# Two-block transformer kernel: the one-column shift products move to TensorE, and the opening's loads and matmuls are reordered

## The chip, the cores and the metric

The kernel runs on one core of one Trainium2 chip. The metric is the device time of one execution in microseconds (us), lower is better.

## What is computed

Two model blocks on one sequence of 512 tokens and width 1024, all in float32. The change touches only the entry of the first block, where a condition vector `c` of 1024 numbers modulates the input:

```
mod = jax.nn.silu(c) @ w_ada[layer] + b_ada[layer]
shift, scale, gate = jnp.split(mod[:, None, :], 3, axis=-1)
h = rms_norm(x, norm_g[layer]) * (1.0 + scale) + shift
proj = h @ w_in[layer]
```

`w_ada` is 1024 x 3072, so shift, scale and gate have 1024 numbers each. Behind it follow HGRN2 and retention heads, an output product, and the second block (convolution, banded attention, two gated feed-forward layers, norms).

## The kernel before, in words

Activations lie with the feature in the partition: x is eight input blocks (`KC` = 8) of 128 features by 512 tokens, in tile `x`. Each f32 product is made of three fast ones: an operand is split into a rounded high part and the rest, its low part, and TensorE adds high x high, low x high and high x low into one bank (the lines of `dense`, L1354 to L1356). So every input block needs `xa_hi` and `xa_lo`, and every weight tile (128 x 1024, half a megabyte) needs `w_hi` and `w_lo`.

Weight tiles come in a fixed order through four slots (`SLOTS`). SyncE loads slot j again once its low part is made (`load`, L376), ScalarE makes the high part (`w_high`, L480), GpSimd the low part (`w_low`, L416), and TensorE uses the tile with all eight input blocks into bank j of `gps`. Each engine's order is written out by hand; nothing is scheduled by a planner. A semaphore is all that ties engines together, and each engine executes its own list strictly in order.

The opening, up to the loop over head pairs:

- SyncE issues in one queue: x's first half, modulation piece 0, x's second half, pieces 1 and 2, weight tile 0, piece 3, tile 1, piece 4, tile 2, pieces 5 to 7, tile 3, constants. A modulation piece is 1 MB and holds, for one input block, the weights of its scale and of its shift, both turned so that an output feature is a partition. ScalarE's queue loads `c` spread over all partitions (`c_wide`) and the table of vectors `vec`.
- ScalarE squares the input blocks (L499), TensorE sums them over the features with a matrix of ones (L1392), ScalarE makes the inverse root `rstd` (L504, L505).
- VectorE makes silu(c) wide (L892), then for each block in `modulation(c)` two products with a running sum over 1024 elements (L897), scale and shift, and the gain (L901); `scaled_input(c)` is x times gain times `rstd` (L910). The first three scaled inputs stand behind the third block's products.
- ScalarE adds the shift in place (L533) and copies the rounded high part (L534), with the high parts of weight tiles 0 to 2 put in between.
- GpSimd makes the low part of input blocks 0 to 5 (L423) and of weight tiles 0 to 2 (L416) in turns; VectorE makes the low part of blocks 6 and 7 (L916). The semaphore `x_ready` counts finished blocks.
- TensorE has weight tiles 0 to 2 in work at once: for blocks 0 to 4 one group of three matmuls per tile and block, then blocks 5 to 7 of tile 0, of tile 1, of tile 2. Then tile 3, and the products of the first head pair.

The first head pair then runs ScalarE's sigmoid of tiles 0 to 3 (L583, L587; the first stands behind two table loads), VectorE's forget gate, key and clamp (L1044, L1047, L1048), ScalarE's log (L590), VectorE's running sums (L1055) and level exponents (L960 to L963), ScalarE's exponentials and copies (L552 to L613), and further weight tiles. TensorE goes from tile 3 to token matmuls (L1383), tiles 6 and 7, the level products (L1451), and the next token matmuls, which need two weight tiles whose low parts GpSimd makes late.

Of the kernel before, what the change touches and what calls it, by code (L numbers as in the profile page):

```python
# [16 lines left out]
F32 = mybir.dt.float32  # L17
# [113 lines left out]
def program(nc, weights, ada_in, c_in, xT, vec_in, sinks_in, rel_in, ret_tab, lvl_in, eye_in, tri_in, hot_in, ident_in,  # L131
            rel_scratch, outT):
    ctx = ExitStack()
    with ctx:
        def sb(name, shape, dt=F32, where=ctx):
            return where.enter_context(nc.sbuf_tensor(name, shape, dt))

        def sem(name):
            return ctx.enter_context(nc.semaphore(name))
# [17 lines left out]
        eps_col = sb("eps_col", [P, 1])  # L157
        mod = sb("mod", [P, 3 * KC])
        conv_gain = sb("conv_gain", [P, KC])
        r_col = sb("r_col", [P, 2, NT])  # L160
        sq = sb("sq", [P, 2, T])
        lnv = sb("lnv", [P, T])
# [78 lines left out]

        gps = ctx.enter_context(nc.psum_tensor("gps", [P, SLOTS, T], F32))
        aps = ctx.enter_context(nc.psum_tensor("aps", [P, 4, T], F32))

# [21 lines left out]
        made = sem("made")  # L266
        lb_shift = sem("lb_shift")
        lb_exp = sem("lb_exp")
        mod_ready = sem("mod_ready")

        sq_ready = sem("sq_ready")
        sq_used = sem("sq_used")
# [61 lines left out]
        def vcol(name, c=0):  # L334
            return vec[:, VEC[name] + c:VEC[name] + c + 1]
# [37 lines left out]
        @block.sync  # L373
        def _(sp):
            def load(I, j):
                sp.dma_start(w_raw[:, j, :], weights[bass.ds(I * SLOTS + j, 1)].rearrange("a p c -> p (a c)"))\  # L376
                  .then_inc(raw_in[j], 16)

            for c in range(KC):  # L380
                if c < 2:
                    k = slice(c * KC // 2, (c + 1) * KC // 2)
                    sp.dma_start(x0[:, k, :], xT.rearrange("(k p) t -> p k t", p=P)[:, k, :]).then_inc(x_in[c], 16)
# [24 lines left out]
        def _(pool):  # L408
# [64 lines left out]
        def _(act):  # L473
# [35 lines left out]
                nc.scalar.mul(dst[:, c, :], res[:, c, :], gain(c)).then_inc(xh_ready, 1)  # L509

            act.dma_start(c_wide[:, 0, :], c_in.to_broadcast([P, D])).then_inc(c_loaded, 16)
            act.dma_start(vec[:], vec_in).then_inc(vec_loaded, 16)

            nc.scalar.preload_act_table(ACT.Sigmoid)
            for c in range(KC):
# [3 lines left out]
                if c == KC // 2 - 1:  # L521
# [318 lines left out]
        def _(dve):  # L840
# [30 lines left out]
            def gain_low(b, c, gain, hi, lo):  # L871
# [16 lines left out]
            own.done(TT(conv_gain[:], vec[:, VEC["final_g"]:VEC["final_g"] + KC], vec[:, VEC["norm_mix"]:VEC["norm_mix"] + KC],  # L888
                        ALU.mult))

            dve.wait_ge(c_wide_ready, 1)
            own.done(TT(c_wide[:, 0, :], c_wide[:, 0, :], c_wide[:, 1, :], ALU.mult))  # L892

            def modulation(c):
                dve.wait_ge(ada_loaded[c], 16)
                for n, col in ((2 * c, KC + c), (2 * c + 1, c)):
                    own.mark(nc.vector.tensor_tensor_reduce(  # L897
                        ada_w[:, n, :], ada_w[:, n, :], c_wide[:, 0, :], op0=ALU.mult, op1=ALU.add, scale=1.0,
                        scalar=vcol("b_ada", col), accum_out=mod[:, col:col + 1]))
                own.wait()  # L900
                own.mark(STT(mix_gain[:, c:c + 1], mod[:, KC + c:KC + c + 1], 1.0, vcol("norm_g", c), ALU.add, ALU.mult))  # L901

            def scaled_input(c):

                if c == 0:
                    dve.wait_ge(rstd_ready, RMS_MIX + 1)
                if c >= 4:
                    dve.wait_ge(x_ready, c - 3)
                own.wait()
                STT(hbuf[:, c % 4, :], x0[:, c, :], mix_gain[:, c:c + 1], rstd[:], ALU.mult, ALU.mult).then_inc(h_ready, 1)  # L910

            def input_low(c):

                dve.wait_ge(xh_ready, c + 1)
                dve.wait_ge(x_ready, c)
                TT(xa_lo[:, c, :], hbuf[:, c % 4, :], xa_hi[:, c, :].bitcast(F32), ALU.subtract).then_inc(x_ready, 1)  # L916

            for c in range(KC):
                modulation(c)

                if c >= 2:
                    for n in range(0, 3) if c == 2 else (c,):
                        scaled_input(n)
            for c in range(KC - LAST_LOW, KC):
# [410 lines left out]
        def _(pe):  # L1335
# [80 lines left out]
            for c in range(KC):  # L1416
                sum_squares(RMS_MIX, c)

            for k in range(KC - 3):
                for c in range(3):  # L1420
                    dense(START["pairs"], c, xa, operand=x_wait(X_MIX) if c == 0 else None, part=(k, k + 1))
            for c in range(3):
                dense(START["pairs"], c, xa, operand=x_wait(X_MIX) if c == 0 else None, part=(KC - 3, KC))

            def pair(p):
# [335 lines left out]

def ada_chunks(w_ada):

    order = [n for c in range(KC) for n in (KC + c, c)]
    return np.stack([np.ascontiguousarray(w_ada[:, c * P:(c + 1) * P].T) for c in order])

def shape_constants():
# [70 lines left out]
```

## Time and profile before

| | before |
|---|---|
| median of 3 runs | 1764.28 us (1763.45 to 1764.39) |
| profiled execution, its own time | 1762.87 us |
| its span in the trace | 1760.9 us |
| TensorE busy, share of the span | 97% |
| VectorE, ScalarE, GpSimd busy | 48%, 44%, 39% |
| mean granted TensorE clock | 0.987 of full speed |

The span runs from the first to the last instruction in the trace; the execution's own time has 2.0 us more around it. Busy shares are averages over the whole span; the first 100 us, in which the change lies, look otherwise. TensorE's granted clock has two levels here, 1.2 GHz (0.5 in the views) and 2.4 GHz (1.0); a stretch with a value in between holds a switch from one to the other.

### The profile page before, as it was taken

Reading aid. Unit: us, or ns where it says so; the run is one execution under the profiler, and the core shown is the slowest. Engines: PE = TensorE matmul, PEld = TensorE weight load, DVE = VectorE, ACT = ScalarE, POOL = GpSimd, SP = SyncE. Lnnn points to the kernel's source line nnn. Section 1 sums busy time; section 2 is a strip of 40 time slices with the busy share of each in tenths; the row PEclk is TensorE's granted clock in tenths of the full one; section 3 lists DMA queues with packets and bytes.
Section 4 is the critical chain, followed back from the end, with each engine's and each line's share of the span. In section 5 each row is a group of like instructions: output and inputs, shape, how many; then the busy total and the mean of one; then the engine's idle time right before and its main releaser. Section 6 shows DMA issues by size and latency. Waiting matters only on the chain.

```text
span 1760.9 us, 22392 instructions
## 1 busy us (share of the span) xinstructions
PE 1699.5 (97%) x8181; PEld 1382.8 (79%) x8181; DVE 842.7 (48%) x1327; ACT 766.3 (44%) x1187; POOL 678.8 (39%) x281
## 2 busy tenths in 40 slices
PE   4899999999999999998999999999999999999997
PEld 2787887887887678884888888888887888888885
DVE  7894585485486438995322122125466322122123
ACT  4553553453553556456443222225576443222222
POOL 3342342342333424321344444445322444444442
PEclk7999999999999999998999999999999999999999
DMA  8221331322322337300232223223211332223221
GB/s 353 98 95 49 107 98 58 108 88 66 107 80 75 109 74 177 120 1 24 84 108 97 94 95 102 89 95 120 72 58 48 99 99 104 92 97 98 95 95 60
DMA packets 49877, 166.85 MB, mean 95 GB/s; under 512 B 4988, under 2 KB 9629, under 8 KB 49309
## 3 DMA queue, kind: packets, MB, share of 16 engines
q1 hardware_dynamic: 43696, 153.74, 25.7%
q10 hardware_dynamic: 6124, 12.33, 3.0%
q8 instruction: 39, 0.64, 0.2%
q14 instruction: 18, 0.14, 0.0%
HBM read 160.81 MB, written 5.24 MB: 94 GB/s over the span
## 4 chain that ended last, share of the span: by engine, by line
PE 84%; DVE 7%; ACT 4%; issue 3%; POOL 2%; DMA 0%; ACTq 0%; DVEq 0%; POOLq 0%
PE gps L1354 23%; PE gps L1356 23%; PE gps L1355 23%; PE aps L1495 2%; POOL w_lo L416 2%; DVE ada_w L897 1%; PE gps L1576 1%; PE gps L1578 1%; PE gps L1577 1%; PE gps L1383 1%; PE gps L1384 1%; PE gps L1385 1%; PE aps L1477 1%; PE aps L1628 1%; DVE cum L1055 1%
## 5 line engine op out<-in xcount | busy, mean ns | idle before, releaser
L416 POOL TENSOR_TENSOR w_lo<-w_raw,w_hi 128x1024 fp32r<-128x1024 f32 x260 | 651.2, 2508 | 986.7 <-ACT w_hi L480 986.6
L1354 PE MATMUL gps<-xa_hi,w_hi 128*128 128x512 f32 x1152 | 461.1, 400 | 20.8 <-POOL xa_lo L423 12.9
L1355 PE MATMUL gps<-xa_lo,w_hi 128*128 128x512 f32 x1152 | 451.0, 392 | 0.0
L1356 PE MATMUL gps<-xa_hi,w_lo 128*128 128x512 f32 x1152 | 451.0, 391 | 0.0
L480 ACT CAST w_hi<-w_raw 128x1024 fp32r<-128x1024 f32 x260 | 270.7, 1044 | 154.9 <-PE gps L1356 136.8
L1354 PE MATMUL gps<-xb_hi,w_hi 128*128 128x512 f32 x736 | 291.5, 396 | 2.4 <-issue 1.2
L1356 PE MATMUL gps<-xb_hi,w_lo 128*128 128x512 f32 x736 | 288.2, 392 | 0.0
L1355 PE MATMUL gps<-xb_lo,w_hi 128*128 128x512 f32 x736 | 286.3, 389 | 0.0
L1354 PEld LDWEIGHTS gps<-xa_hi,w_hi 128*128 128x128 f32 x1152 | 217.7, 189 | 72.8 <-issue 16.6
L1355 PEld LDWEIGHTS gps<-xa_lo,w_hi 128*128 128x128 f32 x1152 | 218.0, 189 | 46.3 <-issue 3.1
L1356 PEld LDWEIGHTS gps<-xa_hi,w_lo 128*128 128x128 f32 x1152 | 217.7, 189 | 46.1
L1354 PEld LDWEIGHTS gps<-xb_hi,w_hi 128*128 128x128 f32 x736 | 138.3, 188 | 33.2 <-issue 3.6
L1356 PEld LDWEIGHTS gps<-xb_hi,w_lo 128*128 128x128 f32 x736 | 138.2, 188 | 32.1
L1355 PEld LDWEIGHTS gps<-xb_lo,w_hi 128*128 128x128 f32 x736 | 138.2, 188 | 30.5 <-issue 0.5
L1259 DVE TENSOR_TENSOR hbuf<-gps,rstd 128x512 f32<-128x512 f32 x44 | 30.4, 692 | 202.7 <-PE gps L1356 202.7
L1202 DVE SCALAR_TENSOR_TENSOR aps<-glu,vec,aps 128x512 f32<-128x512 f32 x145 | 99.5, 751 | 1.0
L1271 DVE TENSOR_TENSOR res<-gps,res 128x512 f32 x32 | 22.1, 692 | 143.8 <-PE gps L1356 143.8
L1258 DVE TENSOR_TENSOR sq<-gps,rstd 128x512 f32<-128x512 f32 x44 | 30.4, 692 | 120.9 <-PE gps L1356 105.6
L769 ACT ACTIVATE sq<-sq 128x512 f32<-128x512 f32 x44 | 27.8, 633 | 117.8 <-DVE sq L1258 117.7
L1383 PE MATMUL gps<-w_hi,xa_hi 128*128 128x256 f32 x256 | 72.7, 284 | 2.7 <-POOL w_lo L416 2.7
L1384 PE MATMUL gps<-w_hi,xa_lo 128*128 128x256 f32 x256 | 72.5, 283 | 0.0
L1385 PE MATMUL gps<-w_lo,xa_hi 128*128 128x256 f32 x256 | 72.4, 283 | 0.0
(248 smaller groups left out, 2029.9 us busy)
## 6 DMA issues: line engine op xcount, KB each, us to landing
w_raw<-weights_dram SPq DMA_DIRECT2D x268, 512.0 KB, 3.3
ada_w<-ada_in_dram SPq DMA_DIRECT2D x8, 1024.0 KB, 16.0
gates<-ret_tab_dram ACTq DMA_DIRECT2D x4, 1024.0 KB, 6.5
rel_scratch_dram<-rel_rows ACTq DMA_DIRECT2D x1, 3072.0 KB, 34.6
x<-xT_dram SPq DMA_DIRECT2D x2, 1024.0 KB, 10.5
res<-xT_dram ACTq DMA_DIRECT2D x1, 2048.0 KB, 8.4
bias<-rel_scratch_dram ACTq DMA_DIRECT2D x1, 2048.0 KB, 10.0
outT_dram<-y SPq DMA_DIRECT2D x8, 256.0 KB, 2.1
```

Source lines behind the costliest of these rows:

```text
L416: TT(w_lo[:, j, :], w_raw[:, j, :], w_hi[:, j, :].bitcast(F32), ALU.subtract).then_inc(lo_ready[j], 1)
L480: nc.scalar.copy(w_hi[:, j, :], w_raw[:, j, :]).then_inc(hi_ready[j], 1)
L1202: made_at[c] = own.mark(STT(bank, src, w, bank, ALU.mult, ALU.add))
L1258: TT(sq[:, m, :], full(I, 2 * m), rstd[:], ALU.mult).then_inc(evicted[2 * m], 1)
L1259: TT(h, full(I, 2 * m + 1), rstd[:], ALU.mult).then_inc(evicted[2 * m + 1], 1)
L1354: mm(gps[:, j, :], w_hi[:, j, w], x[0][:, k, :], start=k == 0, stop=False)
L1355: mm(gps[:, j, :], w_hi[:, j, w], x[1][:, k, :], start=False, stop=False)
L1356: last = mm(gps[:, j, :], w_lo[:, j, w], x[0][:, k, :], start=False, stop=k == blocks - 1)
L1383: mm(out, x[0][:, k, tok], wh, start=k == 0, stop=False)
L1384: mm(out, x[1][:, k, tok], wh, start=False, stop=False)
L1385: last = mm(out, x[0][:, k, tok], wl, start=False, stop=k == KC - 1)
L1495: last = mm(b[:, j * P:], val[:, j, r, e * P:(e + 1) * P], at_x[:, j * (T + P):(j + 1) * T], start=j == 0, stop=j == NT - 1)
```

## The change

1. **Shift on TensorE.** The shift half of each modulation piece is now stored unturned, as eight 128x128 blocks. VectorE makes a small silu(c) column tile `c_col` (128 x 8) from `vec`, and TensorE forms the shift of one block with eight f32 matmuls whose moving operand is one column (`shift(c)`). The results go to column 0 of banks 1, 2, 3 of `aps` and bank 3 of `gps`, in turns (`shift_at`). ScalarE adds the bias into `mod` with a one-column activation.
2. **One pass less on ScalarE, all low parts on VectorE.** ScalarE writes `xa_hi` directly from the scaled input plus shift; `hbuf` keeps the value without shift. VectorE makes the low part of all eight blocks as (hbuf + shift) - xa_hi. GpSimd makes only weight low parts in the opening.
3. **Loads.** Both halves of x are issued ahead of the first modulation piece, the weight tiles 0 to 2 behind pieces 2, 4 and 6, and `vec` ahead of `c_wide`. ScalarE makes the high parts of tiles 1 and 2 later, in front of blocks 4 and 6.
4. **Order.** VectorE runs the scale products four blocks ahead, and scaled inputs three ahead. TensorE's opening interleaves shift groups and matmuls.

```diff
+        shift_at = [aps[:, 1, 0:1], aps[:, 2, 0:1], aps[:, 3, 0:1], gps[:, 3, 0:1]]
...
+            for c in range(2):
+                k = slice(c * KC // 2, (c + 1) * KC // 2)
+                sp.dma_start(x0[:, k, :], xT.rearrange("(k p) t -> p k t", p=P)[:, k, :]).then_inc(x_in[c], 16)
             for c in range(KC):
-                if c < 2:
...
                 sp.dma_start(ada_w[:, 2 * c:2 * c + 2, :], ada_in[2 * c:2 * c + 2].rearrange("c p k -> p c k"))\
                   .then_inc(ada_loaded[c], 16)
-                if 2 <= c < 5:
-                    load(0, c - 2)
+                if c in (2, 4, 6):
+                    load(0, c // 2 - 1)
...
-            for c in range(KC - LAST_LOW):
-                if c < 3:
-                    w_low(0, c)
-                pool.wait_ge(xh_ready, c + 1)
-                TT(xa_lo[:, c, :], hbuf[:, c % 4, :], xa_hi[:, c, :].bitcast(F32), ALU.subtract).then_inc(x_ready, 1)
+            for c in range(3):
+                w_low(0, c)
...
             for c in range(KC):
-                if c < 3:
-                    w_high(0, c)
+                if c in (0, 4, 6):
+                    w_high(0, max(0, c // 2 - 1))
+                act.wait_ge(shift_full, c + 1)
+                own.mark(nc.scalar.activation(mod[:, c:c + 1], shift_at[c % len(shift_at)], ACT.Identity, bias=vcol("b_ada", c)))
                 act.wait_ge(h_ready, c + 1)
-                own.done(nc.scalar.activation(hbuf[:, c % 4, :], hbuf[:, c % 4, :], ACT.Identity, bias=mod[:, c:c + 1]))
-                nc.scalar.copy(xa_hi[:, c, :], hbuf[:, c % 4, :]).then_inc(xh_ready, 1)
+                own.wait()
+                nc.scalar.activation(xa_hi[:, c, :], hbuf[:, c % 4, :], ACT.Identity, bias=mod[:, c:c + 1]).then_inc(xh_ready, 1)
...
-                TT(xa_lo[:, c, :], hbuf[:, c % 4, :], xa_hi[:, c, :].bitcast(F32), ALU.subtract).then_inc(x_ready, 1)
+                STT(xa_lo[:, c, :], hbuf[:, c % 4, :], mod[:, c:c + 1], xa_hi[:, c, :].bitcast(F32), ALU.add, ALU.subtract)\
+                    .then_inc(x_ready, 1)
+
+            gain_at = {c: modulation(c) for c in range(4)}
+            for c in range(3):
+                scaled_input(c)
             for c in range(KC):
-                modulation(c)
...
+                if c + 4 < KC:
+                    gain_at[c + 4] = modulation(c + 4)
+                input_low(c)
+                if c + 3 < KC:
+                    scaled_input(c + 3)
...
+            def shift(c):
+
+                pe.wait_ge(ada_loaded[c], 16)
+                if c >= len(shift_at):
+                    pe.wait_ge(xh_ready, c - len(shift_at) + 1)
+                for k in range(KC):
+                    last = mm(shift_at[c % len(shift_at)], ada_w[:, 2 * c + 1, k * P:(k + 1) * P], c_col[:, 0, k:k + 1],
+                              start=k == 0, stop=k == KC - 1)
+                last.then_inc(shift_full, 1)
...
+            for c in range(5):
+                shift(c)
+            opening(0, 0, 2)
+            shift(5)
+            opening(0, 2, 4)
+            shift(6)
+            opening(1, 0, 4)
+            shift(7)
+            opening(0, 4, 5)
+            opening(1, 4, 5)
+            opening(2, 0, 5)
+            for k in range(5, KC):
+                for c in range(3):
+                    opening(c, k, k + 1)
```

`opening(t, k0, k1)` is `dense` of weight tile t with input blocks k0 to k1 - 1.

TensorE, first order rows of the opening, before. Tile 0, 1 and 2 each take a group of three matmuls with one input block; no other matmul stands between the sums and these.

```order
L1392 MATMUL aps<-sq,ones 128x512 [waits sq_ready] x7
L1354 MATMUL gps<-xa_hi,w_hi 128x512 [waits x_ready,evicted0,lo_ready0]
L1355 MATMUL gps<-xa_lo,w_hi 128x512
L1356 MATMUL gps<-xa_hi,w_lo 128x512
L1354 MATMUL gps<-xa_hi,w_hi 128x512 [waits evicted1,lo_ready1]
L1355 MATMUL gps<-xa_lo,w_hi 128x512
L1356 MATMUL gps<-xa_hi,w_lo 128x512
L1354 MATMUL gps<-xa_hi,w_hi 128x512 [waits evicted2,lo_ready2]
```

The same engine in the changed program, from the last matmuls of input block 3 with tile 0 on: shift group 6 behind them, then tile 1.

```order
L1362 MATMUL gps<-xa_hi,w_hi 128x512 [waits x_ready]
L1363 MATMUL gps<-xa_lo,w_hi 128x512
L1364 MATMUL gps<-xa_hi,w_lo 128x512
L1433 MATMUL aps<-c_col,ada_w 128x1 [waits xh_ready,ada_loaded6]
L1433 MATMUL aps<-c_col,ada_w 128x1 x7
L1362 MATMUL gps<-xa_hi,w_hi 128x512 [waits evicted1,lo_ready1]
```

Shift groups stand between matmuls that need an input block each, and tile 1 starts only behind shift group 6.

VectorE before, one input block: two products (each with a short row that reads the running sum), the gain, the scaled input.

```order
L897 ISA ada_w,mod<-ada_w,c_wide,vec 128x1024 [waits ada_loaded4]
L897 ISA mod 128x1
L897 ISA ada_w,mod<-ada_w,c_wide,vec 128x1024
L897 ISA mod 128x1
L901 SCALAR_TENSOR_TENSOR mix_gain<-mod,vec 128x1 [waits dve_own]
L910 SCALAR_TENSOR_TENSOR hbuf<-x,mix_gain,rstd 128x512 [waits dve_own,x_ready]
```

And in the changed program: one product, and the low part of an earlier block, which waits for ScalarE's high part.

```order
L904 ISA ada_w,mod<-ada_w,c_wide,vec 128x1024 [waits ada_loaded7]
L904 ISA mod 128x1
L907 SCALAR_TENSOR_TENSOR mix_gain<-mod,vec 128x1 [waits dve_own]
L922 SCALAR_TENSOR_TENSOR xa_lo<-hbuf,mod,xa_hi 128x512 [waits xh_ready]
L917 SCALAR_TENSOR_TENSOR hbuf<-x,mix_gain,rstd 128x512 [waits dve_own,x_ready]
```

One product per block is gone and one low part has come; the product of block 7 now stands ahead of the low part of block 3.

## Rows read from the trace of the kernel before

**Rows 1.** The page's first part: busy time, share of the span, instructions.

```profile
PE 1699.5 (97%) x8181; PEld 1382.8 (79%) x8181; DVE 842.7 (48%) x1327; ACT 766.3 (44%) x1187; POOL 678.8 (39%) x281
```

**Rows 2.** Chain of waits in order of time, 0 to 130 us: start, us, what.

```profile
55.98 0.70 DVE xa_lo L916
...
72.26 1.07 ACT forget L590
```

**Rows 3.** TensorE's timeline: start, us, line, operation, idle before and releaser.

```profile
31.33 0.77 PE L1354 MATMUL gps<-xa_hi,w_hi 128*128 128x512 f32 x1 [11.54 <-POOL xa_lo L423]
...
38.52 0.80 PE L1354 MATMUL gps<-xa_hi,w_hi 128*128 128x512 f32 x1 [2.34 <-POOL w_lo L416]
...
51.79 0.50 PE L1354 MATMUL gps<-xa_hi,w_hi 128*128 128x512 f32 x1 [1.31 <-POOL xa_lo L423]
...
56.73 0.80 PE L1354 MATMUL gps<-xa_hi,w_hi 128*128 128x512 f32 x1 [3.98 <-DVE xa_lo L916]
...
59.27 0.63 PE L1356 MATMUL gps<-xa_hi,w_lo 128*128 128x512 f32 x1
59.70 0.63 PE L1354 MATMUL gps<-xa_hi,w_hi 128*128 128x512 f32 x1
...
64.03 0.39 PE L1354 MATMUL gps<-xa_hi,w_hi 128*128 128x512 f32 x1
64.26 0.39 PE L1355 MATMUL gps<-xa_lo,w_hi 128*128 128x512 f32 x1
```

**Rows 4.** Stretches of 1 us: length, busy of PE to POOL, PEclk, DMA.

```profile
24.00:25.00 1.00, 0.00 (x0) 0.00 (x0) 0.96 (x3) 0.00 (x0) 1.00 (x1) 0.52 1.04 430
44.00:45.00 1.00, 1.00 (x5) 0.83 (x4) 1.00 (x3) 0.97 (x2) 0.00 (x0) 0.74 0.04 8
61.00:62.00 1.00, 1.00 (x5) 0.82 (x4) 0.09 (x1) 0.99 (x3) 1.00 (x1) 0.70 0.00 0
```

**Rows 5.** VectorE: summary of L897 (ns min/median/max, first and last start), timeline rows.

```profile
L897 DVE CUSTOM_DVE_ANT_0 ada_w<-ada_w,c_wide,vec x16: 1277/1281/3359, 16.7 to 53.7; 128x1024 f32<-128x1024 f32 x16
...
24.49 2.17 DVE L901 SCALAR_TENSOR_TENSOR mix_gain<-mod,vec 128x1 f32<-128x1 f32 x1
...
68.29 2.77 DVE L1048 TENSOR_SCALAR forget<-forget 128x1024 f32<-128x1024 f32 x1
```

**Rows 6.** GpSimd's timeline.

```profile
23.67 2.98 POOL L416 TENSOR_TENSOR w_lo<-w_raw,w_hi 128x1024 fp32r<-128x1024 f32 x1 [23.22 <-ACT w_hi L480]
...
62.76 7.75 POOL L416 TENSOR_TENSOR w_lo<-w_raw,w_hi 128x1024 fp32r<-128x1024 f32 x3 [0.47 <-ACT w_hi L480]
```

**Rows 7.** Modulation pieces: issue ns, first and last issue, and us to landing.

```profile
L384 SPq DMA_DIRECT2D ada_w<-ada_in_dram x8: 436/1147/2302, 1.3 to 17.7; - x8
...
DMA to landing us min/median/max: 10.4/16.0/17.7
```

**Rows 8.** One-column f32 matmuls (two records each), and weight loads of the first sums.

```profile
1233.29 0.36 PE L1408 MATMUL aps<-ones,sq 128*128 128x1 f32 x2
1233.52 0.36 PE L1407 MATMUL aps<-ones,lnv 128*128 128x1 f32 x2
...
L1392 PEld LDWEIGHTS aps<-sq,ones x16: 186/190/337, 10.0 to 18.8; 128*128 128x128 f32 x16
```

**Rows 9.** ScalarE's timeline.

```profile
22.46 0.20 ACT L528 ACTIVATE lbt<-lbt 128x16 f32<-128x16 f32 x1
...
61.15 0.60 ACT L583 ACTIVATE forget<-gps 128x512 f32<-128x512 f32 x1
...
70.35 0.60 ACT L587 ACTIVATE sq<-gps 128x512 f32<-128x512 f32 x1 [3.90 <-PE gps L1356]
...
92.78 0.59 ACT L610 COPY rqk<-gps 128x512 f32<-128x512 f32 x1 [0.34 <-PE gps L1356]
```

**Rows 10.** TensorE's timeline before the restart.

```profile
92.58 6.36 PE L1451 MATMUL aps<-qt,kt 128*128 128x64 f32 x56
99.62 0.35 PE L1383 MATMUL gps<-w_hi,xa_hi 128*128 128x256 f32 x1 [0.68 <-POOL w_lo L416]
```

More of the change, by code:

```diff
@@ L159, in program @@
         conv_gain = sb("conv_gain", [P, KC])
+        c_col = sb("c_col", [P, 2, KC])
         r_col = sb("r_col", [P, 2, NT])
@@ L268, in program @@
         lb_exp = sem("lb_exp")
-        mod_ready = sem("mod_ready")
+        c_sig = sem("c_sig")
+        c_col_ready = sem("c_col_ready")
+        shift_full = sem("shift_full")
         sq_ready = sem("sq_ready")
@@ L377, in load @@
                   .then_inc(raw_in[j], 16)
+            for c in range(2):
+                k = slice(c * KC // 2, (c + 1) * KC // 2)
+                sp.dma_start(x0[:, k, :], xT.rearrange("(k p) t -> p k t", p=P)[:, k, :]).then_inc(x_in[c], 16)
             for c in range(KC):
-                if c < 2:
-                    k = slice(c * KC // 2, (c + 1) * KC // 2)
-                    sp.dma_start(x0[:, k, :], xT.rearrange("(k p) t -> p k t", p=P)[:, k, :]).then_inc(x_in[c], 16)
                 sp.dma_start(ada_w[:, 2 * c:2 * c + 2, :], ada_in[2 * c:2 * c + 2].rearrange("c p k -> p c k"))\
                   .then_inc(ada_loaded[c], 16)
-                if 2 <= c < 5:
-                    load(0, c - 2)
+                if c in (2, 4, 6):
+                    load(0, c // 2 - 1)
             load(0, 3)
@@ L509, in gain_high @@
                 nc.scalar.mul(dst[:, c, :], res[:, c, :], gain(c)).then_inc(xh_ready, 1)
+            act.dma_start(vec[:], vec_in).then_inc(vec_loaded, 16)
             act.dma_start(c_wide[:, 0, :], c_in.to_broadcast([P, D])).then_inc(c_loaded, 16)
-            act.dma_start(vec[:], vec_in).then_inc(vec_loaded, 16)
             nc.scalar.preload_act_table(ACT.Sigmoid)
+            act.wait_ge(vec_loaded, 16)
+            nc.scalar.activation(c_col[:, 1, :], vec[:, VEC["c"]:VEC["c"] + KC], ACT.Sigmoid).then_inc(c_sig, 1)
             for c in range(KC):
@@ L520, in _ @@
                 rms_square(RMS_MIX, c, x0[:, c, :])
-                if c == KC // 2 - 1:
+                if c == 1:
                     act.wait_ge(c_loaded, 16)
@@ L889, in _ @@
                         ALU.mult))
+            dve.wait_ge(c_sig, 1)
+            TT(c_col[:, 0, :], vec[:, VEC["c"]:VEC["c"] + KC], c_col[:, 1, :], ALU.mult).then_inc(c_col_ready, 1)
             dve.wait_ge(c_wide_ready, 1)
@@ L895, in modulation @@
                 dve.wait_ge(ada_loaded[c], 16)
[L896 to L901, printed above, removed]
+                col = KC + c
+                own.done(nc.vector.tensor_tensor_reduce(
+                    ada_w[:, 2 * c, :], ada_w[:, 2 * c, :], c_wide[:, 0, :], op0=ALU.mult, op1=ALU.add, scale=1.0,
+                    scalar=vcol("b_ada", col), accum_out=mod[:, col:col + 1]))
+                own.mark(STT(mix_gain[:, c:c + 1], mod[:, col:col + 1], 1.0, vcol("norm_g", c), ALU.add, ALU.mult))
+                return own.local
             def scaled_input(c):
@@ L908, in scaled_input @@
                     dve.wait_ge(x_ready, c - 3)
-                own.wait()
+                own.wait(gain_at[c])
                 STT(hbuf[:, c % 4, :], x0[:, c, :], mix_gain[:, c:c + 1], rstd[:], ALU.mult, ALU.mult).then_inc(h_ready, 1)
@@ L914, in input_low @@
                 dve.wait_ge(xh_ready, c + 1)
-                dve.wait_ge(x_ready, c)
-                TT(xa_lo[:, c, :], hbuf[:, c % 4, :], xa_hi[:, c, :].bitcast(F32), ALU.subtract).then_inc(x_ready, 1)
-            for c in range(KC):
-                modulation(c)
[L921 to L924, printed above, removed]
+                STT(xa_lo[:, c, :], hbuf[:, c % 4, :], mod[:, c:c + 1], xa_hi[:, c, :].bitcast(F32), ALU.add, ALU.subtract)\
[3 more added lines that the diff above has]
+                scaled_input(c)
+            for c in range(KC):
+                if c + 4 < KC:
+                    gain_at[c + 4] = modulation(c + 4)
                 input_low(c)
+                if c + 3 < KC:
+                    scaled_input(c + 3)
             own.done(nc.vector.tensor_copy(silu_c, c_wide[:, 0, :]))
@@ L1417, in _, with opening @@
                 sum_squares(RMS_MIX, c)
-            for k in range(KC - 3):
+            def shift(c):
[6 more added lines that the diff above has]
+                last.then_inc(shift_full, 1)
+            def opening(c, k0, k1):
+                dense(START["pairs"], c, xa, operand=x_wait(X_MIX) if c == 0 else None, part=(k0, k1))
+            pe.wait_ge(c_col_ready, 1)
+            for c in range(5):
[10 more added lines that the diff above has]
+            for k in range(5, KC):
                 for c in range(3):
-                    dense(START["pairs"], c, xa, operand=x_wait(X_MIX) if c == 0 else None, part=(k, k + 1))
-            for c in range(3):
-                dense(START["pairs"], c, xa, operand=x_wait(X_MIX) if c == 0 else None, part=(KC - 3, KC))
+                    opening(c, k, k + 1)
             def pair(p):
@@ L1763, in ada_chunks @@
 def ada_chunks(w_ada):
-    order = [n for c in range(KC) for n in (KC + c, c)]
-    return np.stack([np.ascontiguousarray(w_ada[:, c * P:(c + 1) * P].T) for c in order])
+    return np.stack([m for c in range(KC) for m in (np.ascontiguousarray(w_ada[:, (KC + c) * P:(KC + c + 1) * P].T),
+                                                    chunk(w_ada[:, c * P:(c + 1) * P]))])
 def shape_constants():
```

## The prediction

> **What bounds the kernel now.** I read the page first: TensorE is busy in 97% of the span [rows 1], so a change pays only where TensorE stands idle or runs at its lower clock, and the idle time lies in the opening. The chain of waits in order of time comes next [rows 2]: up to the last low part it waited for, at 55.98 us, it is almost all VectorE (products with the modulation weights, gains, scaled inputs), then TensorE, then ScalarE and VectorE again from the log activation at 72.26 us, until GpSimd's low part of a weight tile lets TensorE go on at 99.62 us [rows 10]. Behind that TensorE's row of matmuls is the bound, and whatever is won or lost by 99.62 us is carried to the end unchanged. So the question is how much earlier TensorE restarts at that place.
>
> TensorE's timeline [rows 3] shows the opening: lone groups of three matmuls while it waits for inputs, and two long bursts, from 38.52 and from 56.73 us. The clock view [rows 4] shows what gaps cost: the granted clock falls to 1.2 GHz in the stretch 24 to 25 us, after the last work at 19.8 (31.33 less 11.54); a burst brings it back to 2.4 GHz in 44 to 45 us; it falls again in the next gap and returns in 61 to 62. Matmuls of 512 columns follow each other every 0.43 us at 1.2 GHz (59.27 to 59.70) and every 0.23 at 2.4 GHz (64.03 to 64.26).
>
> **What VectorE pays.** Per input block: two products of 1.28 us (1.20 from start to start), a gain of 0.13 and a scaled input of 0.68, some 3.3 us, or 26 for eight. It took from 16.7 to 55.98, since it shares something with GpSimd: the gain of one column takes 2.17 us at 24.49 and ends where GpSimd's operation ends, and the longest product takes 3.36 [rows 5, 6]. They take turns: a GpSimd weight operation costs VectorE about 2.25 us, one on an input block about 1.15. Nine such operations (three weights, six inputs) run before.
>
> **The change, part by part.**
>
> *Loads.* No modulation piece but the first has more bytes ahead of it than before. Before, piece 0 landed at 1.3 + 10.4 = 11.7 and piece 7 at 17.7 + 17.7 = 35.4 [rows 7]; in between came 9.5 MB (seven pieces, half of x, three weight tiles), so 1 MB takes 2.5 us. That puts x's second half at 14.2 and piece 3 (4.5 MB behind piece 0) at 23.0. Now the first piece and x change places: the second half of x is there at 11.7, piece 0 at 14.2; pieces 4 to 6 lead by one 0.5 MB weight tile, 1.25 us (25.4, 29.2, 31.7); the last stays at 35.4. Alone this is worth 0: the inverse root was ready before 22.5 [rows 9], and VectorE is still busy with products then.
>
> *VectorE* loses eight products (8 x 1.20 = 9.6 us) and six waits for GpSimd (6 x 1.15 = 6.9), and gains six low parts (6 x 0.68 = 4.1). Walked through: product 3 starts on its piece at 23.0 and ends at 24.1. From there to the low part of block 3: products 4 to 7 with gains (4 x 1.38 = 5.5), scaled inputs 0 to 5 (4.1), low parts 0 to 3 (2.7), one gain (0.1), and two GpSimd weight operations in between (4.5): 24.1 + 16.9 = **41.0 us**. The piece due latest (35.4) is there before its product starts at about 39, so VectorE sets this, not the loads.
>
> *ScalarE* drops one pass of 0.62 us per block and adds a one-column activation, which I take at 0.2 like the 16-column one at 22.46 [rows 9]. It waits for VectorE or TensorE in either case: 0.
>
> *TensorE* gains 64 one-column matmuls with 128x128 f32 weights. The same kind stands late in the kernel [rows 8]: pairs follow each other every 0.222 us at 2.4 GHz, so eight are 1.8 us. At 1.2 GHz I take twice that, 3.6, since weight loads of the first sums take from 0.19 to 0.34 us [rows 8]. Bounds for eight: 1.8 and 3.6. The first five groups lie where TensorE stood idle (19.8 to 31.3): 0. Shift group 6 stands behind the fourth block's matmuls of weight tile 0, and shift group 7 behind twelve more. So after 41.0 us the order holds: 3 matmuls, group 6, 12 matmuls, group 7, and 42 more up to the end of tile 0. The last input block needs ScalarE and VectorE behind group 7 (about 2 us), which the 21 matmuls in between cover. At 2.4 GHz: 57 x 0.23 = 13.1, plus 3.6, plus 0.3 for latencies: tile 0 ends at 58.0. But TensorE did little between 28 and 41 us, in groups as thin as those before 38.52, so I start at 1.2 GHz. The two bursts before ran 5.9 and 4.7 us until the clock rose [rows 3, 4]; half of that is lost, 2.3 to 2.9. I take 2.9, because one-column matmuls stand in this burst: tile 0 ends at **60.9 us**.
>
> The Trainium skill (TensorE: Matmul & The Clock Gate, LDWEIGHTS) gives the time of a weight load as its columns over 1.2 GHz, whatever the array's clock. Worked out from it, group 6 would cost 1.8 us at either clock, and tile 0 would end some 1.5 us earlier than in my sum; the loads of 0.34 and 0.19 us [rows 8] speak against it.
>
> *Downstream.* ScalarE's first sigmoid of a tile started at 61.15, held by a table load and not by tile 0, which TensorE had finished at 59.7, where tile 1's matmuls go on [rows 3, 9]. These table loads now come behind the last input block, at 54 to 58 us, and are out of the way. The three tiles end 0.7 us apart instead of one by one. From the first sigmoid to the restart at 99.62 it took 38.5 us. GpSimd's three weight operations [rows 6] follow the first sigmoid and hold VectorE's three operations up to its clamp, which ended at 71.06 [rows 5], 9.9 us behind that sigmoid. This stays. What shortens: the log activation waited for the fourth tile (sigmoid at 70.35, then a table load, log at 72.26 [rows 2, 9]), 11.1 us behind. Now tile 3 ends at 60.9 + 1.4 + 5.5, the table is loaded 8.8 us behind, and the clamp at 9.9 decides: 1.1 saved. A wait of 0.34 us for a tile at 92.78 [rows 9] goes as well. So the restart is 37.0 us behind the first sigmoid: 60.9 + 37.0 = 97.9 against 99.62, or **-1.7 us**. TensorE itself would be there at 60.9 + 1.4 + 34.2 = 96.5 (before, tile 2 ended 24 matmuls ahead of 70.2, at 64.7, and the level products end at 98.9 [rows 9, 10]): most of its gain of 2.4 us turns into a longer wait for that weight tile.
>
> The sum is made against the profiled execution, 1762.87 us, which is 1.4 below the median of the three runs, 1764.28. From the median: 1764.28 - 1.7 = **1762.6**.
>
> **The rivals.** A measurement of this kernel can tell about 0.2% from no change, 3.5 us.
>
> *The clock stays up.* If one-column matmuls count as work, TensorE works without a long gap from 10 to 28 us and the clock may be at 2.4 GHz, or return at once, at 41.0. Tile 0 ends at 58.0, the restart is at 95.0, 4.6 us earlier: 1759.7. For it: the stretch of 64-column matmuls from 92.58 kept the clock. Against it: three matmuls at 51.79 did not, and between 31 and 38 three at a time did not raise it. The Trainium skill (TensorE: Matmul & The Clock Gate, What's actually happening) says that the clock follows how busy the engine has been, and speaks of no size of matmul; by that this rival is the likelier one. No run here shows it for one column.
>
> *The clock comes late.* If the one-column groups do not count, they break the burst into 3, 12 and 42 matmuls, and the rise falls into group 7. Then 1.3 + 3.6 + 5.2 + 2.0 = 12.1 us pass for work that takes 7.1 at the full clock: tile 0 ends at 63.0, the restart at 100.0: +0.4, or 1764.7.
>
> *Slower: the clock comes only in the last burst.* The 15 matmuls and two groups all run at 1.2 GHz (1.3 + 3.6 + 5.2 + 3.6 = 13.7 us, to 54.7), then the 42 need 5.9 us at 1.2 GHz (14 of them) and 6.4 for the other 28: tile 0 at 67.0, with latencies 67.3, the restart at 104.3: +4.7, or 1769.0. It decides once 12 matmuls in a row (5.2 us) no longer raise the clock; that this is near the 4.7 and 5.9 us of the bursts speaks for it, that both rose speaks against.
>
> *It doesn't relieve VectorE.* Its walk may hold more turns with GpSimd than two, since the third weight operation comes right behind block 3's low part. One more before it is +2.2 us everywhere: 1764.8.
>
> **How the numbers follow.** Forecast 0.41, clock stays up 0.23, clock late 0.20, VectorE not relieved 0.07, slower 0.09. Around the forecast the price of the clock (2.3 to 3.6) and the landings leave 1.5 us, on one side of 3.5 alone. Faster by over 0.2% is the first rival, 0.23; slower the third, 0.09; the rest, 0.68, is within 0.2%. The range goes from 1759.5, just below the first rival, to 1766.0, above the two rivals near no change; it leaves out the slower one and outliers.
>
> **What would show it.** VectorE's low part of block 3 ends near 41; the granted clock in 41 to 54 us tells the rivals apart; one-column matmuls follow at 0.22 or 0.44 us; the first sigmoid of a tile starts at 60.9; the clamp ends 9.9 behind it; and TensorE's wait before the token matmuls grows from 0.7 to about 1.4 us. The prediction is wrong if the restart is not near 97.9, or if the time behind it changes.

## The result, and the profile after

The changed kernel took **1775.94 us** (median of 7 executions, 1770.21 to 1779.04), the kernel before 1764.28 beside it (7 executions, 1762.14 to 1766.84): a ratio of **1.0063, 95% interval 1.0052 to 1.0074**. It is slower by 11.7 us, outside the range of the prediction (1759.5 to 1766.0) and past every rival. The profiled execution has a span of 1777.2 us and took 1779.04, 3.1 above the median.

The page's first part, as in [rows 1]:

```profile
PE 1736.1 (98%) x8309; PEld 1411.1 (79%) x8309; DVE 830.6 (47%) x1318; ACT 763.2 (43%) x1188; POOL 661.9 (37%) x275
```

TensorE has 128 more records (64 one-column matmuls of two records) and is busy 36.6 us longer. In the opening that is idle time turned into work, but only some 22 us (90.57 us busy up to 102, against 68.20 up to 100 before). The rest is time that the same work takes longer.

**The opening came out nearly as walked through.** TensorE's timeline after, columns as in [rows 3]; the x48 are three groups of eight, two records each:

```profile
18.52 5.42 PE L1433 MATMUL aps<-c_col,ada_w 128*128 128x1 f32 x48
23.80 3.28 PE L1433 MATMUL gps<-c_col,ada_w 128*128 128x1 f32 x16
27.79 3.54 PE L1433 MATMUL aps<-c_col,ada_w 128*128 128x1 f32 x16 [0.71 <-ACT xa_hi L539]
34.49 3.41 PE L1433 MATMUL aps<-c_col,ada_w 128*128 128x1 f32 x16
...
40.59 0.80 PE L1362 MATMUL gps<-xa_hi,w_hi 128*128 128x512 f32 x1 [1.08 <-DVE xa_lo L922]
...
42.04 3.41 PE L1433 MATMUL aps<-c_col,ada_w 128*128 128x1 f32 x16
...
50.58 2.24 PE L1433 MATMUL gps<-c_col,ada_w 128*128 128x1 f32 x16
```

VectorE's timeline (start, us, line, operation) has block 3's low part and, later, the clamp; ScalarE's has the first sigmoid and the log:

```profile
39.80 0.74 DVE L922 SCALAR_TENSOR_TENSOR xa_lo<-hbuf,mod,xa_hi 128x512 fp32r<-128x512 f32 x1
...
69.67 2.78 DVE L1056 TENSOR_SCALAR forget<-forget 128x1024 f32<-128x1024 f32 x1
```

```profile
62.52 0.60 ACT L588 ACTIVATE forget<-gps 128x512 f32<-128x512 f32 x1 [4.92 <-PE gps L1364]
...
72.48 1.06 ACT L595 ACTIVATE forget<-forget 128x1024 f32<-128x1024 f32 x1 [1.26 <-DVE forget L1056]
```

The low part ends at 40.54 (forecast 41.0). The clock was late: stretches of the trace after (columns as in [rows 4]) show it falling at 24 us and rising only in 51 to 52, during group 7, so the first sigmoid starts at 62.52.

```profile
23.00:24.00 1.00, 1.00 (x11) 1.00 (x11) 1.00 (x1) 0.00 (x0) 1.00 (x1) 1.00 1.03 414
24.00:25.00 1.00, 1.00 (x7) 1.00 (x7) 1.00 (x1) 0.00 (x0) 0.91 (x1) 0.55 1.02 406
...
51.00:52.00 1.00, 1.00 (x8) 1.00 (x9) 0.00 (x0) 0.00 (x0) 0.00 (x0) 0.79 0.00 0
```

The first two of these rows are worth a pause: TensorE is busy for the whole of both stretches, with one-column matmuls, and the granted clock falls all the same, from 1.00 to 0.55.

When it comes back differs from one execution to the next. Five later runs keep this opening instruction for instruction (e1, e3, e5, e6 and e10 below); with the trace after, their six traces have the rise between 48.2 us (e10) and 51.4 (after), and the first sigmoid between 60.82 (e5) and 62.52 (after), 61.65 in the mean.

**The place where the time turns** is the restart. TensorE's timeline after, against [rows 10]:

```profile
91.83 1.89 PE L1482 MATMUL aps<-qt,kt 128*128 128x64 f32 x16
94.40 7.57 PE L1482 MATMUL aps<-qt,kt 128*128 128x64 f32 x40 [0.68 <-DVE kt L979]
101.72 0.56 PE L1391 MATMUL gps<-w_hi,xa_hi 128*128 128x256 f32 x1
```

VectorE's keys, for which it waits, in its timeline before and after:

```profile
90.16 3.96 DVE L971 TENSOR_TENSOR kt<-kt,key 128x1024 f32<-128x1024 f32 x2
```

```profile
90.38 3.96 DVE L979 TENSOR_TENSOR kt<-kt,key 128x1024 f32<-128x1024 f32 x2
```

And stretches of 1, 1 and 9 us there:

```profile
94.00:95.00 1.00, 0.60 (x5) 0.60 (x6) 1.00 (x2) 0.99 (x2) 1.00 (x1) 1.00 0.00 0
95.00:96.00 1.00, 1.00 (x11) 1.00 (x10) 1.00 (x1) 0.96 (x3) 1.00 (x1) 0.90 0.00 0
...
97.00:106.00 9.00, 9.00 (x44) 9.00 (x44) 8.05 (x12) 1.04 (x1) 4.55 (x2) 0.50 0.58 177
```

Before, TensorE came to the 56 level products at 92.58 and went through them without a wait in 6.36 us. Now it comes 0.75 us earlier, does 16 and waits 0.68 us for VectorE's keys. In 95 to 96 the granted clock falls; 40 products take 7.57 us, the first token matmuls run at 1.2 GHz as well, and at 106 us the clock comes back. At tile 3 of the opening TensorE stood 1.0 us ahead of the kernel before (the matmul at 64.7 there starts at 63.7); at the first token matmul it stands 2.1 behind, and when the clock is back, 4.0.

**The last part of the loss has no event at all.** Taken on the same matmul of both traces, the one after is 4.0 us behind from 107 to 580 us, 5.5 at 620, 7.8 at 800, 9.0 at 870 and 15.9 at 1700. Steps of 1.5 and 1.2 us in it are falls of the clock (below); the rest, 2.2 us between 620 and 800 and 6.9 between 870 and 1700, or 9.1 in all, comes little by little with the clock at 1.00, wherever TensorE multiplies with xb_hi and xb_lo, the input tiles of the second block (first at 638 us). TensorE's timeline, two matmuls that stand 30 apart, before and then after:

```profile
1021.86 0.39 PE L1354 MATMUL gps<-xb_hi,w_hi 128*128 128x512 f32 x1
...
1028.72 0.39 PE L1354 MATMUL gps<-xb_hi,w_hi 128*128 128x512 f32 x1
```

```profile
1021.89 0.40 PE L1364 MATMUL gps<-xb_hi,w_lo 128*128 128x512 f32 x1
...
1028.89 0.40 PE L1364 MATMUL gps<-xb_hi,w_lo 128*128 128x512 f32 x1
```

### The profile page after: what moved, and what is told of

It is laid out like the page before. It is cut to its first block, busy times and chain, and to the rows that moved or that the text cites. A ratio compares the mean times of both kernels' runs of the same rounds, so it can differ in the third digit from the quotient of the medians.

```text
span 1777.2 us, 22645 instructions
## 1 busy us (share of the span) xinstructions
PE 1736.1 (98%) x8309; PEld 1411.1 (79%) x8309; DVE 830.6 (47%) x1318; ACT 763.2 (43%) x1188; POOL 661.9 (37%) x275
## 4 chain that ended last, share of the span: by engine, by line
PE 86%; DVE 5%; ACT 4%; issue 3%; POOL 2%; DMA 1%; SPq 0%; ACTq 0%; DVEq 0%; POOLq 0%
PE gps L1362 23%; PE gps L1364 23%; PE gps L1363 23%; PE aps L1526 2%; PE aps L1482 2%; POOL w_lo L420 1%; PE gps L1607 1%; PE gps L1608 1%; PE gps L1609 1%; PE gps L1391 1%; PE gps L1393 1%; PE gps L1392 1%; PE aps L1508 1%; DMA ada_w<-ada_in_dram 1%; PE aps L1659 1%
## 5 line engine op out<-in xcount | busy, mean ns | idle before, releaser
L1363 PE MATMUL gps<-xb_lo,w_hi 128*128 128x512 f32 x736 | 290.5, 395 | 0.0
```

Source lines behind the costliest of these rows:

```text
L1363: mm(gps[:, j, :], w_hi[:, j, w], x[1][:, k, :], start=False, stop=False)
```

## The experiments

**The address alone, and c_col out of the way.** Four kernels. e1 is the change with c_col allocated behind the modulation weights, where it moves nothing:

```diff
-        c_col = sb("c_col", [P, 2, KC])
...
+        c_col = sb("c_col", [P, 2, KC], where=ada_mem)
```

> The changed kernel with the small tile c_col placed behind c_wide, where it moves no other tile; everything else as changed. Theory A (the 64 bytes that c_col puts in front of all later tiles make TensorE's reads of the second block slower): the 512-column matmuls of the second block follow each other every 0.2289 us again instead of 0.2324 to 0.2334, and 8 to 10 us of the loss go: 1763 to 1768 us, the upper end if the clock still falls at the level products near 96 us. Theory B (the new order or the one-column matmuls slow something all along): about 1776 us, pitch 0.232 or more.

e2 is the kernel before with an unused tile of the same size in c_col's place:

```diff
+        sb("gap", [P, 2, KC])
```

> The kernel before with nothing but an unused tile of 64 bytes per partition at the place of c_col. Theory A: 1770 to 1774 us, pitch of the second block's matmuls 0.232 to 0.233, the opening unchanged to 99.6 us. Theory B: 1764 us and 0.2289.

e3 is the change, e4 the kernel before, each with the padding ahead of the second block 64 bytes smaller:

```diff
-XB_PAD = 240
+XB_PAD = 224
```

> The changed kernel with the unused tile in front of the second block's tiles 64 bytes shorter (240 to 224 numbers), so that only the second block's tiles lie where they lay before and the first block's stay moved. Theory A, with the cost in the second block's tiles: 1763 to 1768 us like the run with c_col aside. If the cost were in the first block's tiles: 1772 us or more. Theory B: 1776 us.

> The kernel before with the second block's tiles 64 bytes lower (xb_hi at a multiple of 2048 bytes, where xa_hi also lies). If the start of the moving operand alone decides, its matmuls come every 0.2267 us like those on xa_hi, some 4 to 5 us faster than before (1760 us). If it is the distance between two tiles that are used together, anything from 1758 to 1775. Theory B: 1764 us.

Measured (ratios to the kernel before in the same session, 1764.8 us):

| run | median us | ratio, 95% interval | xb_hi behind xa_hi, bytes past a multiple of 256 | spacing on xb |
|---|---|---|---|---|
| e1 | 1768.98 | 1.0018 (1.0009 to 1.0027) | 64 | 0.2289 |
| e2 | 1773.87 | 1.0052 (1.0039 to 1.0065) | 128 | 0.2333 |
| e3 | 1768.81 | 1.0015 (1.0002 to 1.0027) | 64 | 0.2289 |
| e4 | 1760.78 | 0.9980 (0.9969 to 0.9991) | 0 | 0.2267 |

(Spacing: mean of starts on xb between 1010 and 1070 us.) An unused tile of 64 bytes costs the kernel before 9 us; that is most of the loss, and no instruction is needed for it. On the same matmul its trace loses the same as the one after, 2.2 us between 620 and 800 and 6.9 between 870 and 1700. e1 and e3 get 7 us back by two different edits. But some 4 us stay, and in the profiled e1 the fall of the clock at the levels is there (0.50 in 95 to 105 us); in e2 it is not, since that kernel has the old opening.

**The fall at the levels.** e5 is e1 with three matmuls of 512 columns put into TensorE's wait for the keys. They go into the bank that the next level product overwrites, so nothing is left out:

```diff
+                        b = bank(u + n)
+                        if isinstance(p, int) and e == 0 and n == 1:
+                            for _ in range(FILL):
+                                mm(b[:, :], xa_hi[:, 0, 0:P], xa_hi[:, 1, :], start=True, stop=True)
```

> The kernel of the run that laid the 64-byte column aside (1768.98 us median), with three more matmuls of 512 columns, whose result is overwritten, put into the wait of 0.68 us that stands ahead of the level products of the first chunks (at 93.64 us there). Theory C (the remaining loss of about 4 us is the clock's fall at 94.9 us, brought on by narrow matmuls and a wait): with the wait filled, TensorE's clock stays at 2.4 GHz through the level products in most executions, tokens restart near 97 us instead of 101, and the median is 1763 to 1765 us. Rival D (the fall comes from the narrow level products alone, or from the opening's length): the 10.2 us at half clock stay, and the median is 1769 us, or 1770 with the three matmuls added. Rival E (the 4 us are not of the clock): the fall goes away and the time stays at 1769.

e5 took **1762.63 us** (0.9994, 0.9985 to 1.0003). TensorE's timeline of e5:

```profile
91.85 0.94 PE L1479 MATMUL aps<-xa_hi 128*128 128x512 f32 x3
92.72 4.68 PE L1486 MATMUL aps<-qt,kt 128*128 128x64 f32 x40
97.78 0.36 PE L1392 MATMUL gps<-w_hi,xa_hi 128*128 128x256 f32 x1 [0.38 <-POOL w_lo L421]
```

Stretches of 10 us, e1 and then e5:

```profile
95.00:105.00 10.00, 10.00 (x48) 10.00 (x48) 9.08 (x12) 1.98 (x2) 5.57 (x3) 0.50 0.47 159
```

```profile
95.00:105.00 10.00, 9.62 (x82) 9.51 (x82) 8.90 (x13) 1.05 (x2) 4.84 (x2) 1.00 0.51 159
```

The same 40 products take 4.68 us instead of 7.65 in e1 (from 93.64 us there), and TensorE again waits for GpSimd's weight tile before the restart, as before the change. In e1 nine of twelve executions took 1768.5 to 1770.0 us and three 1763.8 to 1766.2; in e5 nine took 1760.3 to 1763.2 and three 1765.6 to 1766.1. So extra work on TensorE, 0.9 us of it, wins some 5 us: 6.3 between the two medians, but e1 and e5 come from different sessions and chips, and against the kernel before of its own session e1 is 4.2 slower and e5 1.1 faster, which makes 5.2. On the same matmul, e1 loses 5.0 us against the kernel before between 64.7 and 107 us, and e5 0.2. The fall stands in all three traces of the changed kernel without the three matmuls (after, e1, e3), and in none of the five with them (e5, e6, e10, and e7 and e9 with a changed opening; e9 and e10 ran on e1's chip). Two things go at once, the wait and the run of narrow matmuls without a wide one among them; which of the two brings the fall on is not separated.

**Both mended.** e6 is e5 with XB_PAD = 224, so that xb_hi lies a multiple of 2048 bytes behind xa_hi. e7 adds to it another order in the opening: groups 5, 6 and 7 are issued in one row, so that full-size matmuls of pieces 0 and 1 are less broken up.

```diff
             opening(0, 0, 2)
             shift(5)
-            opening(0, 2, 4)
             shift(6)
-            opening(1, 0, 4)
             shift(7)
+            opening(0, 2, 4)
+            opening(1, 0, 4)
```

> The same, with the second block's tiles aligned 16 elements earlier, so that the array xb_hi, TensorE's moving operand in the second block, begins at a multiple of 2048 bytes. Theory A (the spacing of the 512-column matmuls goes by the byte address of the moving operand: 0.2267 us at 0, 0.2289 at 64, 0.2333 at 128 modulo 2048): 0.2267 us in the second block and 4 us under the run beside it, so about 1759 to 1760 us if the fall at 95 us is gone, 1764 to 1765 if it stays. Rival (the spacing follows something else that the gap had shifted): spacing 0.2289 us and the same time as the run beside it.

> The kernel of the run before this one, with the groups 5, 6 and 7 of one-column matmuls issued ahead of the opening's full-size products of pieces 0 and 1, which then run in one stretch. Theory F (one-column matmuls count for nothing in TensorE's clock, so that the two groups among the full-size products keep the clock low until 51.4 us): with one stretch of full-size products the clock rises some 3 us earlier or more, and the first sigmoid starts at 60 to 61.5 us instead of 62.5, with the restart behind the levels 1 to 2 us earlier and a median 1 to 2 us lower. Rival G (the groups do no more than take their own 3.4 us wherever they stand): the clock rises at the same time or later and the first sigmoid stays at 62 to 63 us; no difference.

e6: **1758.47 us** (0.9972, 0.9961 to 0.9983), spacing 0.2267. e7: 1759.53 (0.9974, 0.9965 to 0.9983): no difference. Its clock rises at 51.7 us instead of 50.9 and its first sigmoid starts at 62.41 instead of 61.99, in one trace each; the old order alone gave 48.2 to 51.4. Full-size matmuls run in one row from 45.64 us there, at 1.2 GHz up to 51.7. The earlier rise and the 1 to 2 us of theory F did not come; rival G fits.

**Spacing against address.** e8 and e12 are the kernel before with XB_PAD = 288 and 272, one execution each.

> The kernel before with its second block aligned 32 elements later, which puts xb_hi at 256 modulo 2048 bytes; no instruction is changed. Theory A, if the spacing grows with the distance from the multiple of 2048: at least 0.2333 us between 512-column matmuls of the second block, and 1773 us or more. If it goes by some smaller unit (a multiple of 256 is as good as one of 2048): 0.2267 us and 1760 to 1761 us.

> The kernel before with xb_hi at 192 bytes behind a multiple of 256. If the spacing grows with the distance from the multiple: above 0.2333 us and 1773 us or more. If it goes by the distance to the nearest multiple of 256, either way: 0.2289 us and 1764 us.

e8 (a distance from xa_hi 256 bytes past a multiple of 2048): 0.2267 us and 1758.78. e12 (192 past a multiple of 256): 0.2333 and 1773.08. TensorE's timeline, again 30 spacings, of the kernel before at 0 bytes (e11, below) and of e12:

```profile
1021.97 0.39 PE L1354 MATMUL gps<-xb_hi,w_hi 128*128 128x512 f32 x1
...
1028.77 0.39 PE L1354 MATMUL gps<-xb_hi,w_hi 128*128 128x512 f32 x1
```

```profile
1021.98 0.39 PE L1354 MATMUL gps<-xb_hi,w_hi 128*128 128x512 f32 x1
...
1028.98 0.39 PE L1354 MATMUL gps<-xb_hi,w_hi 128*128 128x512 f32 x1
```

6.80 and 7.00 us. A distance of 256 bytes past a multiple of 2048 is as good as the multiple; 64 past a multiple of 256 costs 0.0022 us a matmul, 128 and 192 past cost 0.0066. Both my forms for 192 (above 128, or as good as 64) were wrong: it is equal to 128. Between these points nothing was measured on xb, and why it is so no run tells.

One thing more stayed open. In all these runs only the second block's tiles move against the weight tiles, so it is not separated whether the moving operand's own address counts or its distance from the weights. The traces show that the moving operand alone is not the whole of it. 96 matmuls of the second block use the tiles the other way round: `w_hi` and `w_lo`, which no run moved, are the moving operand (256 columns), and xb_hi and xb_lo the weights. TensorE's timeline, the first and the last of them, before and in e4:

```profile
1240.45 0.28 PE L1383 MATMUL gps<-w_hi,xb_hi 128*128 128x256 f32 x1
...
1251.23 0.28 PE L1385 MATMUL gps<-w_lo,xb_hi 128*128 128x256 f32 x1
```

```profile
1239.13 0.28 PE L1383 MATMUL gps<-w_hi,xb_hi 128*128 128x256 f32 x1
...
1250.52 0.28 PE L1385 MATMUL gps<-w_lo,xb_hi 128*128 128x256 f32 x1
```

95 spacings take 10.78 us before and 11.39 in e4, and 11.27 after: 0.1135 at 64, 0.1199 at 0, 0.1186 at 128; in e12, at 192, it is 0.1178. Here the distance that is best for the 512-column matmuls is the slowest, though with 96 matmuls it costs only 0.6 us.

**The opening kept warm?** e9 is e6 with 14 matmuls of 256 columns among the one-column ones:

```diff
+                    if c < 7 and k % 4 == 3:
+                        mm(gps[:, 2, 0:256], ada_w[:, 2 * c + 1, 0:P], ada_w[:, 2 * c + 1, 0:256], start=True, stop=True)
```

> The kernel of the filled and aligned run (1758.47 us) with 14 further matmuls of 256 columns in 32-bit floats among the one-column matmuls of the first seven groups, two a group; their result is never read. Theory H (the opening's clock falls at 23.6 us because TensorE then does one-column matmuls only, and each narrow group costs 3.4 us instead of 1.8 for that): the clock stays at 2.4 GHz through the opening or comes back before 45 us; tile 0 is then bound by the last pieces' low parts (VectorE ends them near 54.7) and the first sigmoid starts at 58 to 60 us instead of 62.0, and the median is 1755 to 1757 us. Rival I (what is won in the opening is lost behind it, as TensorE waits for the keys or for GpSimd's low parts of the weights ahead of the token matmuls): the first sigmoid is early but the median stays at 1758 to 1759. Rival J (the clock falls all the same): the first sigmoid comes at 64 us or later and the median is 1760 to 1762.

1764.25 us (0.9995, 0.9980 to 1.0011): rival J, though slower than the 1760 to 1762 it gave. TensorE, stretches of 1 us in e9:

```profile
21.00:22.00 1.00, 1.00 (x11) 0.97 (x9) 0.00 (x0) 0.34 (x2) 0.74 (x1) 1.00 1.06 434
22.00:23.00 1.00, 1.00 (x5) 0.82 (x5) 0.96 (x1) 0.00 (x0) 1.00 (x1) 0.53 0.99 410
```

The clock falls at 22 us all the same, the added work runs at half speed, and the first sigmoid starts at 65.87. One execution of twelve took 1755.46 us with a mean clock of 0.991, the highest of all runs here, so the clock may stay up at times; that was not profiled. What the opening would need to keep it up remains open.

**What the change itself is worth.** The mended kernel and the kernel before, both aligned, side by side:

> The filled and aligned kernel once more, beside the kernel before with the same alignment, to tell what the change itself is worth when neither the address nor the fall at the levels disturbs it. My theory (the opening is won by about 1 us at the restart behind the levels, and carried to the end): 1758.5 us, 1 to 2 us under the run beside it. Rival (nothing is carried): no difference.

> The kernel before with its second block's tiles aligned 16 elements earlier, once more: 1760 to 1761 us by the theory that the change is worth 1 to 2 us, 1758.5 us by the rival that it is worth nothing. Spacing 0.2267 us in the second block by both.

e10: **1757.75 us** (0.9964, 0.9951 to 0.9977). e11: 1759.33 (0.9973, 0.9962 to 0.9984). The difference is 1.6 us in one session. Between e6 and e4 it was 2.3, and 1.2 with each taken against the kernel before of its own session. The sign is the same both times, but the intervals overlap, so it is not shown that the change pays. The alignment does: 4 to 5 us in the kernel before, with one number changed. e10 and e6 beat both kernels of this case.

## Why the prediction was wrong

*VectorE's walk* was right: product 3 started when its piece landed, at 22.83 us (forecast 23.0), and block 3's low part ended at 40.54, forecast 41.0. No load set anything between the two.

*The price of one-column matmuls* was right: eight took 1.81 us at 2.4 GHz (5.42 for three groups) and 3.41 at 1.2 GHz, forecast 1.8 and 3.6. The Trainium skill (TensorE: Matmul & The Clock Gate, LDWEIGHTS) gives a weight load as its columns over 1.2 GHz, with no second value for the other clock. By that eight of them, 16 loads of 128 columns, would take an estimated 1.7 us at either clock; the rows at the higher clock fit this, those at the lower one do not.

*The clock in the opening* was mis-sized, by up to 1.6 us. I took 2.9 us for one burst and a rise in the middle of it. In the trace after the rise came in group 7, which was the rival "the clock comes late", to half a microsecond: first sigmoid 62.52, rival 63.0, forecast 60.9. But in e5 and e10, with the same opening, it started at 60.82 and 60.89, and the mean of six traces, 61.65, lies between the two. So neither of the two is refuted, and what decides between them no run tells. I had given the forecast twice that rival's chance. That the clock stays up is refuted: it fell in the stretch 24 to 25, and in 22 to 23 in e9, with TensorE busy in 1.00 of either. The Trainium skill (same page, What's actually happening), by which the clock follows how busy the engine has been, made that rival look likelier; these rows do not agree with it.

*The path behind the first sigmoid* was right in every run without the fall: 97.78 - 60.82 = 36.96 us in e5, and 36.9 in e6 (61.99 to 98.91), forecast 37.0. The clamp ended at 72.45 in the trace after, 9.9 us behind the sigmoid, forecast 9.9, and the log came right behind it. VectorE's keys ended 0.2 us later than before (94.34 against 94.12), as a sigmoid that is 1.37 us late and a path that is 1.1 shorter give.

*The first step that failed* is "most of its gain of 2.4 us turns into a longer wait for that weight tile". I had worked out that TensorE would be early, and put its whole wait at the place where it waited before. It waits in two places, and the first is inside the level products, for the keys. Behind that wait the clock fell, and the wait of 0.68 us became a loss of some 5: on the same matmul TensorE goes from 1.0 ahead at 64.7 us to 4.0 behind at 107, where 1.7 ahead was forecast for the restart. The row of narrow matmuls at 92.58 that "kept the clock" [rows 10] was read as a sign that narrow work holds it; it had only shown this for 56 products that come without a wait.

*The second, and the larger*, is "whatever is won or lost by 99.62 us is carried to the end unchanged". It rests on TensorE's row being the same row with the same spacing. An allocation of 64 bytes changed the spacing of 2208 matmuls, from 0.2289 to 0.2333 where they follow each other: 9 us of the 11.7, shown by e2 without any of the change's instructions. I had read the new tile in the diff only as an operand. None of my rivals had a price outside the opening.

Put together, from the medians, each run against the kernel before of its own session: the address is +9.1 (e2), and the change without it +4.2 (e1), which is -1.1 for the change with the wait filled (e5) and +5.2 for the fall at the levels (e1 less e5). 9.1 + 4.2 = 13.3, measured 11.7; the 1.6 between them is not explained, and is of the size by which medians move. With the first two taken out the change gives -1.1 (e5), forecast -1.7, but with the wait for GpSimd at 0.38 us instead of grown to 1.4, and the interval of e5 (0.9985 to 1.0003) holds no change as well. That its median, 1762.63, meets the forecast 1762.6 is luck: the median of the kernel before alone moved between 1763.69 and 1764.8 us from session to session.

## What to carry to other kernels

Work out the addresses of TensorE's operands before and after any edit that allocates something, from the start of the partition and not from the first tile. Here the 512-column matmuls were fastest where the moving tile lay a multiple of 256 bytes from the weight tiles, which was not a multiple of 256 itself but 128 past one. No view has a row for it, only the spacing of starts: so compare that in two traces, and try one or two paddings. When TensorE is made early at a wait, find the first wait that it meets, not the one it used to end in, and ask what the clock is fed with there; a few wide matmuls whose result is overwritten can be cheaper than standing still. And do not count on one-column matmuls to keep the clock: in the trace after it fell at 24.1 us with TensorE busy with them, and in the trace before it fell at 24.0 with TensorE idle since 19.8.

## What was not expected of the hardware

- The spacing of 512-column matmuls went with where the moving tile lay against the weight tiles: 0.2267 us at a multiple of 256 bytes, 0.2289 at 64 past, 0.2333 at 128 and at 192 past, at a granted clock of 1.00. With the same tile as the weights and 256 columns moving it was 0.1199, 0.1135, 0.1186 and 0.1178 at 0, 64, 128 and 192.
- The granted clock fell from 1.00 to 0.55 in the stretch 24 to 25 us with TensorE busy in 1.00 of it, and from 1.00 to 0.53 in 22 to 23 in e9, where wider matmuls stood among the narrow ones.
- Three wasted matmuls (0.94 us) in a wait of 0.68 us won 6.3 us between the medians (1768.98 to 1762.63), 5.2 with each taken against the kernel before of its session.
